# The first two units of three projections, made by pairs of token tiles in passes of 256 columns, and the mixers' first weights rounded in front of their norm

## The reference

```python
h = rms_norm(x, attn_norm_g)                # norm n1
proj = h @ w_in                             # 1024 x 4608: convolution, q, k, v, gates
u_conv = proj[..., :1024]; q, k, v, gates = ...
...
x = x + hierarchical_moe(...)               # the results of two experts for each token are added
h = rmsnorm(x, norm_mix_pre)                # norm n3
z = h @ w_in_2                              # columns of the four mixers
...
x = x + rmsnorm(y @ w_out_2, norm_mix_post)
h = rmsnorm(x, norm_ffn_pre)                # norm n4
gate, up = split(h @ ffn_w_up, 2)           # 1024 x 5632
f = gelu(causal_conv(gate)) * up
x = x + rmsnorm(f @ ffn_w_down, norm_ffn_post)
```

## Time and profile before

| | |
|---|---|
| time, median of 3 runs | 3218.23 us (3212.55 to 3220.1) |
| the profiled execution's own time | 3222.07 us |
| its span in the trace | 3220.3 us |
| PE busy | 2843.7 us, 88% of the span |
| DVE busy | 1816.1 us, 56% |
| ACT busy | 1343.3 us, 42% |
| POOL busy | 340.8 us, 11% |
| first projection, first unit started to third unit started | 43.0 to 68.0 us |
| mixers' projection, the same | 1533.1 to 1558.6 us |
| feed-forward projection, the same | 2466.5 to 2493.6 us |

### The profile page before, as it was taken

One profiled execution on the slowest core, in us unless ns is written; L12 is line 12 of the kernel. 1 busy time (PEld: TensorE's weight loads), 2 busy tenths in 40 slices (PEclk: granted clock), 3 DMA queues, 4 the chain that ended last, 5 costly groups with the idle time before them and its releaser, 6 DMA issues. The chain is left out here.

```text
span 3220.3 us, 42139 instructions
## 1 busy us (share of the span) xinstructions
PE 2843.7 (88%) x14427; PEld 2356.1 (73%) x14427; DVE 1816.1 (56%) x2255; ACT 1343.3 (42%) x2024; POOL 340.8 (11%) x230
## 2 busy tenths in 40 slices
PE   6999987799599999993999978578796999999997
PEld 5888766677578888882787767466675888887876
DVE  4995427754489999995362546664435333323344
ACT  4123427613178888883322133563335222221232
POOL 1222210010011111112222100002000000000000
PEclk9999998999799999996999977888598999999999
DMA  3112234133199999995122210302032111111122
GB/s 101 37 49 80 81 112 153 50 113 134 73 391 414 417 414 415 413 386 198 53 62 76 72 40 2 131 2 42 12 111 81 50 52 46 47 50 33 49 105 81
DMA packets 247659, 421.03 MB, mean 131 GB/s; under 512 B 33581, under 2 KB 152404, under 8 KB 247540
## 3 DMA queue, kind: packets, MB, share of 16 engines
q1 hardware_dynamic: 218356, 349.89, 29.9%
q10 hardware_dynamic: 20336, 39.59, 3.3%
q0 software_dynamic: 8848, 29.96, 2.8%
HBM read 349.05 MB, written 70.33 MB: 130 GB/s over the span
## 5 line engine op out<-in xcount | busy, mean ns | idle before, releaser
L2151 DVE TENSOR_TENSOR e_w_lo<-e_ring,e_w_hi 128x1024 fp32r<-128x1024 f32 x384 | 447.0, 1221 | 46.7 <-ACT e_w_hi L2078 46.7
L2078 ACT CAST e_w_hi<-e_ring 128x1024 fp32r<-128x1024 f32 x384 | 377.3, 1049 | 35.4 <-PE banks L2011 28.5
L2414 PE MATMUL banks<-h_hi,u_w_hi 128*128 128x512 f32 x672 | 261.5, 389 | 2.1 <-DVE u_w_lo L2457 2.1
L2415 PE MATMUL banks<-h_lo,u_w_hi 128*128 128x512 f32 x672 | 261.4, 389 | 0.0
L2416 PE MATMUL banks<-h_hi,u_w_lo 128*128 128x512 f32 x672 | 261.4, 389 | 0.0
L2009 PE MATMUL banks<-e_w_hi,e_xT_hi 128*128 128x512 f32 x512 | 203.1, 397 | 0.0
L2011 PE MATMUL banks<-e_w_hi,e_xT_lo 128*128 128x512 f32 x512 | 200.2, 391 | 0.0
L2010 PE MATMUL banks<-e_w_lo,e_xT_hi 128*128 128x512 f32 x512 | 199.8, 390 | 0.0
L937 DVE SCALAR_TENSOR_TENSOR conv<-x_first,vectors,conv 128x1024 f32<-128x1024 f32 x120 | 186.9, 1557 | 9.8 <-issue 0.9
L2414 PEld LDWEIGHTS banks<-h_hi,u_w_hi 128*128 128x128 f32 x672 | 126.1, 188 | 28.6 <-DVE u_w_lo L2457 2.5
L2268 PE MATMUL banks<-fd_w_hi,fd_s_hi 128*128 128x512 f32 x352 | 138.4, 393 | 9.6 <-DVE fd_s_lo L2327 8.8
(11 more groups left out here) (593 smaller groups left out, 6732.0 us busy)
## 6 DMA issues: line engine op xcount, KB each, us to landing
e_ring<-in_w_gate_e_dram SPq DMA_DIRECT2D x128, 512.0 KB, 6.1
e_ring<-in_w_up_e_dram SPq DMA_DIRECT2D x128, 512.0 KB, 6.1
e_ring<-in_w_down_e_dram SPq DMA_DIRECT2D x128, 512.0 KB, 5.2
yT<-in_ffn_w_up_dram SPq DMA_DIRECT2D x44, 512.0 KB, 3.8
expert_results<-nothing SPq DMA_DIRECT2D x1, 16384.0 KB
expert_results<-e_y ACTq DMA_DIRECT2D x32, 512.0 KB, 7.6
p_w<-in_w_in_dram SPq DMA_DIRECT2D x24, 512.0 KB, 3.7
fd_w<-in_ffn_w_down_dram SPq DMA_DIRECT2D x44, 256.0 KB, 2.5
```

Of the source, the lines that this page charges most:

```text
L2078: nc.scalar.copy(w_hi[:, part, :], experts.ring[:, slot, :]).then_inc(w_rounded, 1)
L2151: tt(w_lo[:, part, :], experts.ring[:, slot, :], w_hi[:, part, :].bitcast(F32), ALU.subtract).then_inc(w_split, 1)
L2414: nc.tensor.matmul(bank, w_hi[:, up, k, :], h_hi[:, k, tokens], start=(k == 0), stop=False)
L2415: nc.tensor.matmul(bank, w_hi[:, up, k, :], h_lo[:, k, tokens], start=False, stop=False)
```

## The change

`first_units` works by four pairs of token tiles instead of two halves. It first turns four tiles instead of six. Then for each pair q, once 2q + 2 tiles are parted, it makes both units for 256 tokens: 24 matmuls of 256 columns for each unit, and behind each of the first four such passes one of the tiles 4 to 7 is turned. The products of a unit for two pairs lie in the halves of one bank. The signals to ACT come after pairs 1 and 3 (`project_first`, `project_columns`) or after pair 3 alone (`ffn_up`). All three projections call it, and `project_first` and `ffn_up` are otherwise as before. In `CombinedNorm.on_scalar` a square root of a constant column is put in front, and in `project_columns` the fills of weights 0 and 1 move from inside the norm to in front of it.

```diff
     def first_units(self, pe, split, banks, w_hi, w_lo, projected, halves=True):
         mm = self.K.nc.tensor.matmul
-        for t in range(NT - 2):
+        PAIRS = NT // 2
+        for t in range(4):
             self.turn(pe, t)
-        for h in range(2):
-            pe.wait_ge(self.parted, NT // 2 * (h + 1))
+        for q in range(PAIRS):
+            pe.wait_ge(self.parted, 2 * q + 2)
+            tokens = slice(2 * q * P, (2 * q + 2) * P)
             for u in range(2):
-                if h == 0:
+                if q == 0:
                     pe.wait_ge(split, u + 1)
-                bank, tokens = banks(u, h), slice(h * HALF, (h + 1) * HALF)
+                bank = banks(u, q // 2)[:, (q % 2) * 2 * P:(q % 2 + 1) * 2 * P]
                 for k in range(KT):
                     mm(bank, w_hi(u, k), self.hi[:, k, tokens], start=(k == 0), stop=False)
                     mm(bank, w_hi(u, k), self.lo[:, k, tokens], start=False, stop=False)
                     last = mm(bank, w_lo(u, k), self.hi[:, k, tokens], start=False, stop=(k == KT - 1))
-                    if h == 0 and u == 0 and k in (2, 5):
-                        self.turn(pe, NT - 2 + (k == 5))
-                if halves or h == 1:
+                if q + 2 < PAIRS:
+                    self.turn(pe, 2 * q + 4 + u)
+                if q == PAIRS - 1 or (halves and q == PAIRS // 2 - 1):
                     last.then_inc(projected, 1)
...
     def on_scalar(self, act, between={}):            # CombinedNorm
         PAIRS = NT // 2
+        self.K.nc.scalar.activation(self.junk[:, 0:1], self.K.const("ones")[:, 0:1], ACT.Sqrt)
+        act.drain()
         self.square(act, 0)
         self.root(act, 0)
...
-            norm.on_scalar(act, {1: lambda: fill(0), 2: lambda: fill(1)})
+            fill(0)
+            fill(1)
+            norm.on_scalar(act)
```

## The result

The changed kernel took 3232.71 us, median of six runs (3228.77 to 3236.56), beside 3219.18 us for the kernel before in six runs (3212.55 to 3225.63). The ratio is 1.0040, with a 95% interval of 1.0028 to 1.0051: 9 to 16 us slower. The forecast was 3223 us, in a range from 3215 to 3231; the time is 1.7 us above that range, and the likeliest case, a change of less than 0.2%, did not come true. The profiled execution took 3230.29 us with a span of 3228.5 us, 8.2 us more than before; PE was busy for 2844.8 us.

What follows compares the result with a forecast made beforehand. PE, 97 to 98% busy behind each place, was taken as the bound, so third-unit starts shift everything after. +3.3 - 7.0 + 8.6 = +4.9 us gave 3227.0 profiled, 3223.1 as median; range 3215 to 3231.

Steps and rivals of the forecast that it cites:

- the likeliest case, a change of less than 0.2%: Whole kernel: the three terms as worked out, +1 to +6.4 us, within 0.2% of before; chance 0.50.
- The rival by which PE's waits for DVE would take up the delays: Waits at 343.31 and 2958.68 us swallow the first term and 7.8 us of the last: 3212 us; chance 0.07.
- First projection, forecast +3.3: First projection: third unit starts at 71.3 instead of 67.98, as a 2.88 us pass covers the refill; bounds +2, +4.5.
- Mixers' projection, forecast -7.0: Mixers' projection: third unit at 1551.3 instead of 1558.64, less 0.3 for a clock fall; bounds -9 and -5.
- The low parts follow POOL's gathers, over 15 us before they are wanted: Mixers' projection: with fills in front, POOL makes both weights' low parts long before PE needs them.
- The case that had been named, a second load that lands late: Mixers' projection: second load later than 10.1 us holds ACT's squares, lost one for one beyond 1.7 us; within slower's 0.33.
- Feed-forward projection, forecast +8.6: Feed-forward projection: third unit +6.6 us later, plus +2.0 for the low clock; bounds +5 and +10.5.
- Second-pass wait: Feed-forward projection: PE idles 4.0 us for weight 1's low part, then the pass takes 4.6 us at the low clock.
- third-unit wait: Feed-forward projection: PE idles 4.9 us instead of 2.1 before the third unit, for the refill of slot 0.
- low clock behind it: Feed-forward projection: the clock falls at the start of the third unit, costing +2.0 us.
- falls everywhere: Rival: clock falls in all three places, mixers' term -5.2, sum +8.8, 3227 us; chance 0.33, shared with the late second load.
- all upper bounds but one: Range's upper end, 3231 us: stated as a sum of about +10 plus 2 us of measurement scatter.

Runs made afterwards that it cites:

- Experiment 13: Against the kernel before: only the mixers' projection changed, with POOL's low parts of weights 0 and 1 held until DVE's means of pairs 1 and 2; 0.9964, 3208.95 us.
- experiment 4: Against the kernel before: only the two fills and the square root moved in front of the mixers' norm, all units by halves; ratio 1.0001.
- experiment 3: Against the kernel before: pairs in the feed-forward projection alone, the other two by halves, fills and square root not moved; ratio 1.0024.
- experiment 9: Against the kernel before: the whole change, with unit 0's last two passes in front of unit 1's last two; ratio 1.0020.

## Why the prediction was wrong

**The view of what binds: right.** The third units' starts moved everything behind them. The rival by which PE's waits for DVE would take up the delays is refuted: the wait near 343 us is 5.5 us as before, 1400 us on the first projection's 4 us are still there, and the wait near 2958 us is 7.7 instead of 7.8.

**First projection, forecast +3.3: right**, a little small, about +4 over five profiles, inside its bounds. Start, low clock of the first pass (42.44 to 46.93 is 4.49; forecast 4.6), order of passes and refill came as worked out.

**Mixers' projection, forecast -7.0: wrong, -4.6.** The step that failed is "The low parts follow POOL's gathers, over 15 us before they are wanted". They were that early, and so free for PE. But their new place lies beside DVE's mean of pair 1, which stands between ACT's squares and all the scales of that pair, and POOL's operations kept it waiting for 2.4 us. Before, the low parts ran later, from 1530.62 on, and this mean took 0.17 us. I had asked who waits for POOL, and not who runs beside it. Experiment 13 holds only those low parts back and gives the 7.06 us. The case that had been named, a second load that lands late, did occur (ACT's second fill waited until 1500.29), but it was not the cause: in experiment 4 the load landed after 8.9 us, less than before, and the mean took 3.40 us. Its own price is small and near the one that was named, 0.6 us for a landing after 12.4: the mean of pair 1 starts 16.7 to 16.8 us behind DVE's first add in the three profiles with a landing after 12.0 us or more, and 16.3 us on average in the other thirteen, a difference of some 0.4 us.

The Trainium skill states what fits this ("SBUF — State Buffer", section "SBUF: two separate sides"): DVE and GpSimd share a port pair under an exclusive lock, and whoever is second "fully blocks" until the other's instruction is over. The mean's end together with POOL's, in two kernels and with two different lengths (2.56 and 3.40 us), agrees with that. The page names DVE operations in a 2-port mode or with two SBUF inputs, and says that `tensor_scalar`, the mean's operation, can enter such a mode (section "Who interferes with whom"); the mean has one input tensor, and no row shows in which mode it ran. The page speaks of one GpSimd instruction, and here the mean was held over two. That the lock is the mechanism is argued from the page, not shown; that POOL's low parts cause the stall is shown: it stands in all eight profiles with the low parts there, 2.55 to 3.40 us, and in none of the four that hold them back.

**Feed-forward projection, forecast +8.6: right in each step, +9.0 in the traces.** Second-pass wait 3.77 us (forecast 4.0), that pass 4.29 (4.6), third-unit wait 4.96 (4.9), third unit +7.4 to +7.9, less the +0.7 of the halves (+6.6), low clock behind it +1.3 to +2.7 in three profiles (+2.0). That last term has no one size: in the kernel after the low level lasts from 2497.63 to 2503.68, some 14 products, and the starts of the 24 products of this half span 2505.76 - 2497.63 = 8.13 us, before 5.39; in experiment 3 it lasts six products, and they span 6.69.

**The sum.** The forecast's +4.9 becomes +8.4 by the traces: 0.7 from the first term, 2.4 from the mixers', 0.4 from the last. The measured +9 to +16 asks for more. The median lies 9.6 us above the forecast: 3.5 of them are these terms, 2.4 of that the failed step, 1.0 is the base (3218.23 in the three runs that were known, 3219.18 in six), and some 5 us are not placed. Without the failed step the median would be near 3230.3, just inside the range; by itself that step would give only 3225.5. Where the other 5 are I can't say: the parts timed alone add up to less than the whole, and the profiles' drift of 5 us and more in untouched loops hides it. Of the rivals, "falls everywhere" (3227 us) came nearest, and half for the wrong reason: it had -5.2 for the mixers' term, by the clock, where the blocked mean did it. No low phase was seen there behind the two short stretches (0.76 and 1.52 us).

**The range** failed in taking 2 us for the measurement's scatter: its upper end had about +10 for the terms, and the median came at +13.5. That +10 was all three upper bounds together (4.5 - 5 + 10.5), not "all upper bounds but one". The formula that the prediction quotes from the Trainium skill ("TensorE: Matmul & The Clock Gate", section "Back-to-back issue gap") is given there for a matmul by itself, and not for a stream with weight loads as here. The sum used the trace's 0.229 and 0.12 us, so nothing in it rests on that formula.

## What to carry to other kernels

When work moves to another time on GpSimd, look at what VectorE does at that time: a tiny operation in a chain of norms was held here until two GpSimd instructions were over, and a wait that puts the GpSimd work just behind it cost nothing, as that work was still in time. Finer passes pay where PE is waiting for data that arrive piece by piece, and cost where it is not: each turn and each low part that used to be made beside PE's queue can now stand behind a pass in it, so go through the other engines' orders before splitting. Put the low part that the second pass needs ahead of whatever waits for the first pass.

## What the runs showed of the hardware

The price of a 256-column product is now measured at both levels of the clock: they start 0.12 us apart at the high one and (2462.02 - 2459.03) / 14 = 0.214 at the low one, a little under twice.

How short an idle stretch can be before the low clock follows is not settled by one profile. In front of the third unit of the feed-forward projection PE was idle for 4.67 to 4.97 us in four profiles, and the first 24 products took 6.7 to 8.1 us in all of them, between first and last start. It was idle for 2.08 to 2.41 us in twelve: in nine of them the products took 5.3 to 5.4 us, and in three 6.9, one of these the unchanged kernel before, whose first profile had 5.39. The same program then loses 1.55 us there or not. The timeline of PE in that second profile of the kernel before:

```profile
2500.22 0.80 PE L2414 MATMUL banks<-h_hi,u_w_hi 128*128 128x512 f32 x1 [2.10 <-DVE u_w_lo L2457]
...
2503.38 0.51 PE L2415 MATMUL banks<-h_lo,u_w_hi 128*128 128x512 f32 x1
2503.72 0.39 PE L2416 MATMUL banks<-h_hi,u_w_lo 128*128 128x512 f32 x1
```

So a stretch near 2 us can't be counted as safe, and one near 5 us cost the clock in all four profiles here. What tells the two outcomes at 2 us apart stays open. The first product behind a wait does not tell either: behind 3.77 us the fall came ten products later (2469.4), and in experiment 9, behind 2.08 us, after four (2493.27).
